# Forming the sixth input tile's products at a change of layer apart, as old input plus r times output, in an 18-sublayer transformer kernel

## What is computed

```
def rmsnorm(x, w):
    y = xf * rsqrt(mean(xf * xf, axis=-1) + NORM_EPS);  return y * w
def swiglu(x, w_in, w_out):
    g, u = split(x @ w_in, 2);  return (silu(g) * u) @ w_out
for i in range(DEPTH):
    h = h + 0.5 * rmsnorm(swiglu(rmsnorm(h, gn[0]), ffn1_w_in[i], ffn1_w_out[i]), gn[1])
    h = h + rmsnorm(mixer(rmsnorm(h, gn[2])), gn[3])
    h = h + 0.5 * rmsnorm(swiglu(rmsnorm(h, gn[4]), ffn2_w_in[i], ffn2_w_out[i]), gn[5])
```

## Time and profile before

| | us |
|---|---|
| median of 3 runs (lowest to highest) | 3103.48 (3103.17 to 3106.68) |
| the profiled execution's own time | 3105.66 |
| its span | 3103.9 |
| PE busy in the span | 3056.2 (98%) |
| DVE busy | 2252.3 (73%) |
| ACT busy | 1731.4 (56%) |

### The profile page before, as it was taken

One profiled execution on the slowest core, in us unless ns is written; L12 is line 12 of the kernel. 1 busy time (PEld: TensorE's weight loads), 2 busy tenths in 40 slices (PEclk: granted clock), 3 DMA queues, 4 the chain that ended last, 5 costly groups with the idle time before them and its releaser, 6 DMA issues.

```text
span 3103.9 us, 46097 instructions
## 1 busy us (share of the span) xinstructions
PE 3056.2 (98%) x18744; PEld 2702.2 (87%) x18744; DVE 2252.3 (73%) x2670; ACT 1731.4 (56%) x2092; POOL 4.1 (0%) x22
## 2 busy tenths in 40 slices
PE   9999999999999999899999999999999999999998
PEld 7888888888888888788888888888988888888887
DVE  7769775867786775685876977586777775867874
ACT  6556754645664654454655675464634654646653
POOL 0000000000000000000000000000000000000000
PEclk9999999999999999999999999999999999999999
DMA  6543455454355454355454345545433454554453
GB/s 229 188 172 140 157 188 182 179 189 164 135 187 188 173 188 171 143 188 189 176 190 176 136 152 188 189 177 190 175 138 107 177 188 168 192 190 161 163 190 122
DMA packets 75362, 534.87 MB, mean 172 GB/s; under 512 B 8480, under 2 KB 8608, under 8 KB 10784
## 3 DMA queue, kind: packets, MB, share of 16 engines
q1 hardware_dynamic: 75168, 532.07, 47.6%
HBM read 530.99 MB, written 1.05 MB: 171 GB/s over the span
## 4 chain that ended last, share of the span: by engine, by line
PE 93%; DVE 3%; ACT 2%; DMA 1%; issue 0%; DVEq 0%; SPq 0%; ACTq 0%
PE pp L2157 18%; PE pp L2156 18%; PE pp L2158 9%; PE pp L2155 9%; PE pp L2182 4%; PE pm L2157 4%; PE pm L2156 4%; PE pp L2148 3%; PE pp L2150 3%; PE pp L2149 3%; PE pp L2222 2%; PE pp L2184 2%; PE pm L2158 2%; PE pm L2155 2%; PE pp L2330 1%; PE pp L2212 1%
## 5 line engine op out<-in xcount | busy, mean ns | idle before, releaser
L1889 DVE TENSOR_TENSOR wlo<-raw,whi 128x2048 fp32r<-128x2048 f32 x487 | 1113.5, 2289 | 355.9 <-ACT whi L1682 355.2
L1682 ACT ACTIVATE whi<-raw 128x2048 fp32r<-128x2048 f32 x487 | 928.8, 1911 | 275.9 <-DMA raw<-weights 274.9
L2157 PE MATMUL pp<-xs,whi 128*128 128x512 f32 x2176 | 867.1, 398 | 1.9 <-DVE tsum L1969 1.7
L2156 PE MATMUL pp<-xs,whi 128*128 128x512 f32 x2176 | 860.8, 396 | 0.0
L2155 PE MATMUL pp<-xs,wlo 128*128 128x256 f32 x2176 | 605.8, 278 | 0.0
L2158 PE MATMUL pp<-xs,wlo 128*128 128x256 f32 x2176 | 603.6, 277 | 0.0
L1772 ACT ACTIVATE corr<-pp 128x512 f32<-128x512 f32 x320 | 191.0, 597 | 583.2 <-PE pp L2156 558.4
L2155 PEld LDWEIGHTS pp<-xs,wlo 128*128 128x128 f32 x2176 | 408.5, 188 | 99.4
L2158 PEld LDWEIGHTS pp<-xs,wlo 128*128 128x128 f32 x2176 | 409.2, 188 | 92.0
L2157 PEld LDWEIGHTS pp<-xs,whi 128*128 128x128 f32 x2176 | 413.1, 190 | 10.2 <-DVE tsum L1969 8.9
L2156 PEld LDWEIGHTS pp<-xs,whi 128*128 128x128 f32 x2176 | 407.8, 187 | 0.0
(11 more groups left out here) (387 smaller groups left out, 4762.8 us busy)
## 6 DMA issues: line engine op xcount, KB each, us to landing
raw<-weights SPq DMA_DIRECT2D x503, 1024.0 KB, 4.8
raw<-weights SPq DMA_DIRECT2D x8, 256.0 KB, 7.5
h<-x_by_feature SPq DMA_DIRECT2D x4, 256.0 KB, 6.6
out<-h SPq DMA_DIRECT2D x4, 256.0 KB, 2.5
vec<-vectors SPq DMA_DIRECT2D x1, 264.0 KB, 2.8
lamrow<-diff_lambda SPq DMA_DIRECT2D x1, 128.0 KB, 10.6
skiprow<-ssm_d SPq DMA_DIRECT2D x1, 8.0 KB, 12.0
```

Of the source, the lines that this page charges most:

```text
L1682: nc.scalar.activation(whi[:, slot, :], raw[:, slot, :], ACT.Copy).then_inc(sem("weights_hi"), 1)
L1889: v.tensor_tensor(wlo[:, slot, :], raw[:, slot, :], whi[:, slot, :].bitcast(F32), ALU.subtract).then_inc(sem("weights_lo"), 1)
L2156: return mm(bank, whi[:, slot, c:c + P], x_k, start=False, stop=stop)
L2157: mm(bank, whi[:, slot, c:c + P], x_k, start=start, stop=False)
```

## The change

- `fold`, a buffer in the place of `tsum`, takes the sixth tile (`APART` = 5) of the next sublayer's input in two pieces, each as high and low part: the gain times the old `h`, and the gain times the scaled output `upd`, before r is known. DVE makes the first in the old sublayer's read-out (`old_input`), the second after the last squares (`close_sublayer`).
- Behind the last column sum PE forms the old input's product straight into the in-banks of panels 0 and 1 (4 wide, 4 narrow) and the output's product into `pm` banks 0 and 1 (12 narrow). `keep_clock(5)` goes away except before the first sublayer. `first_pair` then adds tiles 0, 1, 2, 3, 4, 6, 7 to the banks; tile 5 is updated and split last.
- DVE adds r times the product from `pm` to the corrected panels 0 and 1 (`add_apart`), in two instructions for each panel.
- In every FFN's opening DVE's steps stand in another order: the split of panel 4 ahead of the first gate, the correction of panel 2 behind it, and the split of panel 6 behind the second hidden tile; on ACT the copy of panel 2 stands ahead of the first hidden tile.
- Pooling: the first group's product goes behind panel 3, the last group's behind the rows (2, 3). HGRN: the splits of the output panels 1 and 2 each one place ahead. The squares of tiles 6 and 7 are added before those of 4 and 5.

```diff
+        fold_offset = nc.sbuf_base
         tsum = sb("tsum", [P, 2, 2 * T])
+        fold = nc.alloc_sbuf_tensor_at("fold", [P, 2, 2 * T], F32R, offset=fold_offset)
+        APART = 5
+        TILES = (0, 1, 2, 3, 4, 6, 7, APART)
...
+            group(0)
             begin(s, 0)
             begin(s, 1)
             rows(s, (y,), (6, 7), ((0, 0), (0, 1), (1, 0), (1, 1)), order, scaled)
             group(1)
             group(2)
             rows(s, (y,), (4, 5), ((0, 0), (0, 1), (1, 0), (1, 1)), order, scaled)
+            rows(s, (y,), (2, 3), ((0, 0), (0, 1), (1, 0), (1, 1)), order, scaled)
             group(3)
-            rows(s, (y,), (2, 3), ((0, 0), (0, 1), (1, 0), (1, 1)), order, scaled)
...
             def hook(p):
                 steps_of(p)
+                if p == 13:
+                    split(s["segs"][1].g0 + 1)
                 if p == 14:
                     nc.scalar.preload_act_table_set("silu_and_others")
                     silu_of(range(3))
-                    split(s["segs"][1].g0 + 1)
+                    split(s["segs"][1].g0 + 2)
...
                 silu_of(0)
-                hidden_of(0)
                 for j in range(1, FF // PC):
                     g = seg.g0 + 2 * j
                     act.wait_ge(sem("panel_done"), g + 1)
                     copy_corr(in_banks[0], 0)
                     if j == 1:
+                        hidden_of(0)
                         split(g + AHEAD - 1)
...
+            def split_apart(s, part, src, ready):
+
+                src, gain = src[:, APART, :], vec[:, APART, s["gain"]:s["gain"] + 1]
+                v.tensor_scalar(fold[:, part, 0:T], src, gain, None, ALU.mult)
+                dve.drain()
+                v.scalar_tensor_tensor(fold[:, part, T:2 * T], src, gain, fold[:, part, 0:T].bitcast(F32),
+                                       ALU.mult, ALU.subtract).then_inc(sem(ready), 1)
...
                 output_squares(s, 1)
+                if nxt is not None:
+                    dve.wait_ge(sem("output_scaled"), 4 * n + APART // 2 + 1)
+                    split_apart(nxt, 1, upd, "output_split")
                 dve.wait_ge(sem("rstd_ready"), 2 * n + 2)
...
                 open_input(seg, s)
                 gate_of(0)
+                add_corr(t2[0], in_banks[0], 0, seg.c0 + 2)
+                if s["n"]:
+                    add_apart(1)
                 hidden_of(0)
-                split(seg.g0 + AHEAD)
                 hidden_lo(0)
                 for j in range(1, FF // PC):
                     g, c = seg.g0 + 2 * j, seg.c0 + 2 * j
-                    add_corr(t2[0], in_banks[0], 0, c)
+                    if j > 1:
+                        add_corr(t2[0], in_banks[0], 0, c)
                     dve.drain()
                     gate_of(j)
+                    split(g + AHEAD - (j == 1))
+                    add_corr(t2[1], in_banks[1], 1, c + 1)
+                    dve.drain()
+                    hidden_of(j)
                     if j == 1:
-                        split(g + AHEAD - 1)
-                    split(g + AHEAD)
-                    add_corr(t2[1], in_banks[1], 1, c + 1)
-                    dve.drain()
-                    hidden_of(j)
+                        split(g + AHEAD)
                     split(g + 1 + AHEAD)
                     hidden_lo(j)
+
+            def add_apart(p):
+
+                scale = rpost[:, :].rearrange("p (a t) -> p a t", a=1).to_broadcast([P, 2, T])
+                v.tensor_tensor(upd[:, 2 * p:2 * p + 2, :], two(pm[:, p, :]), scale, ALU.mult)
+                dve.drain()
+                v.tensor_tensor(t2[p], t2[p], upd[:, 2 * p:2 * p + 2, :], ALU.add)
+                dve.drain()
...
+                dve.drain()
+                if s["kind"] == FFN:
+                    split(seg.g0 + AHEAD)
+                if s["n"]:
+                    add_apart(0)
+                    if s["kind"] != FFN:
+                        add_apart(1)
...
+            def old_input(s):
+
+                if s["n"] + 1 < len(subs):
+                    split_apart(subs[s["n"] + 1], 0, h, "old_input_split")
...
+                tiles = TILES[:KD - 1] if fill else range(KD)
...
+                if fill:
+                    pe.wait_ge(sem("x_lo"), KD * fill + KD)
...
             def first_of(s):
 
-                keep_clock(5 if s["n"] else 7)
+                if s["n"] == 0:
+                    keep_clock(7)
                 first_pair(s["segs"][0], s["fill"])
...
+                seg = nxt["segs"][0]
+                pe.wait_ge(sem("weights_lo"), splits_before[seg.g0] + 2)
+                pe.wait_ge(sem("panel_out"), seg.r0)
+                pe.wait_ge(sem("output_scaled"), 4 * n + 3)
+                pe.wait_ge(sem("old_input_split"), n + 1)
+                old_input_product(nxt, 0)
+                pe.wait_ge(sem("output_scaled"), 4 * n + 4)
+                old_input_product(nxt, 1)
+                pe.wait_ge(sem("output_split"), n + 1)
+                output_product(nxt, 0)
+                output_product(nxt, 1)
```

More of the change, by code:

```diff
@@ L513, in pe_pool @@
             begin, rows, rest = out_products
+            products(s["segs"][0], xs, first=lambda: first_of(s), sums=lambda: column_sums(s), hook=lambda p: None)
             slot = seg.g0 % SLOTS
+            pe.wait_ge(sem(f"raw_landed_{slot}"), landings(seg.g0))
             def group(n):
@@ L527, in scaled @@
                 pe.wait_ge(sem("pool_scaled"), 4 - k // 2)
-            def first_group(p):
-                if p == 2:
-                    pe.wait_ge(sem(f"raw_landed_{slot}"), landings(seg.g0))
-                    group(0)
-            products(s["segs"][0], xs, first=lambda: first_of(s), sums=lambda: column_sums(s), hook=first_group)
+            group(0)
             begin(s, 0)
@@ L934, in act_hgrn @@
             hi_of(3)
-            split(s["segs"][1].g0 + 2)
             split(s["segs"][1].g0 + 3)
@@ L1721, in open_first @@
                         nc.scalar.activation(whi[:, g, quarter(c)], raw[:, g, quarter(c)], ACT.Copy).then_inc(sem("first_hi"), 1)
-                for q in (slice(0, 4), slice(4, 6), slice(6, 8)):
-                    if q.start == 6:
+                for q in (slice(0, 4), slice(6, 8), slice(4, 6)):
+                    if q.start == 4:
                         split(2)
@@ L1727, in open_sublayer @@
             def open_sublayer(s):
-                for k in range(1, KD):
-                    act.wait_ge(sem("h_ready"), KD * (s["n"] - 1) + k + 1)
+                for n, k in list(enumerate(TILES))[1:]:
+                    act.wait_ge(sem("h_ready"), KD * (s["n"] - 1) + n + 1)
                     nc.scalar.activation(xs[:, k, 0:T], h[:, k, :], ACT.Copy, scale=vec[:, k, s["gain"]:s["gain"] + 1]
@@ L1957, in close_sublayer @@
                 hi_of_tile_0(nxt)
-                lo_of_tile(nxt, 0)
+                lo_of_tile(nxt, 0, 0)
                 update(1)
-                for k in range(1, KD):
-                    if k < KD - 1:
-                        update(k + 1)
-                    lo_of_tile(nxt, k)
+                for place in range(1, KD):
+                    if place < KD - 1:
+                        update(TILES[place + 1])
+                    lo_of_tile(nxt, TILES[place], place)
                 dve.drain()
@@ L2040, in read_out @@
                     half, pair = (p + seg.first_half) % 2, p - seg.wide
+                    if closing and pair == 2:
+                        old_input(s)
                     if own_order and p in seg.tokens:
@@ L2181, in rows @@
                             if part == "whi":
-                                e = mm(bank, whi[:, slot, c:c + P], xs[:, k, :], start=(k == 0), stop=(k == KD - 1))
+                                e = mm(bank, whi[:, slot, c:c + P], xs[:, k, :], start=(k == 0 and not fill), stop=(k == KD - 1))
                             else:
@@ L2185, in rows @@
                     return e
-                for k in range(KD - 2):
+                for k in tiles[:-2]:
                     if fill == 0 and k % 2 == 0:
```

38 lines of the change are left out of this document (26 added, 12 removed).

## The result

The changed kernel takes **3143.16 us** (median of 4 runs, 3143.02 to 3145.0), the kernel before 3103.53 beside it: a ratio of 1.0127, 95% interval 1.0113 to 1.0140. It is slower, by 39.6 us. In its profiled execution it took 3143.03 us with a span of 3141.3, where the kernel before had 3105.66 and 3103.9: 37.4 us more in both.

The account below looks back on a forecast made before the run. PE bounds the kernel (93% of the chain); new PE waits for DVE are lost in full. FFNs 32.8, HGRN -1.5, pooling -3.4, REC +1.3, attention and HYB +0.2: +29.4 on 3103.48 gives 3132.9 us, range 3113 to 3147 (83%).

Parts of the forecast that it names:

- the opening FFN: First FFN: no pairs to add, loses only the split's place, which its slack takes; 0.
- The first tiles: At each sublayer change: added PE products replace constants at no cost; panel 2 comes 0.47 us sooner, the rest waits for DVE.
- The constants' rival: At sublayer changes: added products don't fit before 539.36 as a semaphore comes late; 0.5 us each, 17 times, 3141; 3%.
- The FFN's chain: FFN opening: DVE's pairs (1.54 us each) and moved split delay corrections 3 and 4; PE waits 1.88 and 1.57 us.
- Panel 6 starts at 576.94 and not at 573.96: In each FFN but the opening one: panel 6 starts 2.98 us later; times 11 is +32.8 us.
- Mixers: All get both pairs (3.08 us) before read-out: HGRN -1.5, pooling -3.4, REC +1.3, attention and HYB together +0.2.
- pooling: First group behind panel 3 waits 1.7 for 3.96 us, runs at full clock; smaller waits follow; -3.4 us.
- REC: Pairs add 3.08 us before a correction PE already waits for, less some 1.7 of DVE idle; +1.3 us.
- HGRN: PE up to 0.9 us late from the pairs; moved splits end a 1.68 us wait; -0.8 each, two: -1.5.
- The rival of the clock: PE's clock falls after the FFN's new 1.88 us wait, costing 1.26 us 11 times: 3147; 8%.
- the forecast's own signs of being wrong: Correction waits totalling under 20 us (38 forecast), granted clock falling inside an FFN, or pairs outside 1.4 to 1.6 us.
- The skill's shorter pair: DVE's pairs: by the skill page's fixed cycles, a pair 0.13 us shorter, the sum some 3 us lower; not adopted.

Follow-up runs that it names:

- without pairs: The changed kernel without the two pairs of DVE instructions (scale the output's product, add it) in the 11 FFNs, mixers keeping theirs: 3109.04 us (1.0017).
- the order alone: The kernel before with only the changed order of DVE and ACT in the FFN's opening, nothing computed apart: 3114.52 us (1.0035).
- the run without their pairs: The changed kernel without the two pairs of DVE instructions in the 6 mixers, the FFNs keeping theirs: 3131.16 us (1.0092).
- the moves alone: The kernel before with only pooling's first and last groups and HGRN's splits moved as in the change: 3094.52 us (0.9970).

## Why the prediction was right

The forecast was 3132.9 in a range of 3113 to 3147 with slower at 86%; it came to 3143.2. The direction and the mechanism were right, the size 10 us short. Of these, 3.9 are in the FFNs and 4.6 in the mixers, against 0.5 won at the start and in the opening FFN; the remaining 2.2 are no work: the forecast took the profiled execution as 2.2 above the median, and the changed kernel's is not.

- **The first tiles: right.** Added products fit before the low part; PE's wait there fell to 0.27, the wait at panel 2 is 0.9, as said. The constants' rival fell. By medians the parts add up so: FFN pairs 34.1, mixer pairs 12.0, order 10.7, moves -9.9; the measured 39.6 leaves -7.3 for the first tiles, 0.43 at each of 17 changes (0.47 in the forecast). This is what is left over, no run has it by itself, and the even share is in part luck: in the FFNs panel 6 comes 0.56 sooner without pairs than with the order alone (34.59 and 35.15 below), and in the mixers the run without their pairs against that of the moves alone gives 0.3 on average, with nothing to speak of in attention and REC.
- **The FFN's chain: right, nearly to the step.** Counted from the first matmul, the correction of panel 0 comes at 10.37 (10.39 foretold), of panel 3 at 29.67 (29.69), of panel 4 at 36.84 (36.84). The wait at panel 5 is 1.8 (1.88). A pair takes 1.60 and 1.52 us with its drains (559.56 to 561.16, 563.64 to 565.16), and 1.5 in the runs without it (1.54).
- **"Panel 6 starts at 576.94 and not at 573.96": two small slips, +2.98 against +3.34.** PE's timeline of the kernel before, at panel 6, and of the changed one at panel 6 of the FFN that opens at 2035.55, where the clock stayed up:

```profile
573.79 0.39 PE L2157 MATMUL pp<-xs,whi 128*128 128x512 f32 x1
574.03 0.28 PE L2158 MATMUL pp<-xs,wlo 128*128 128x256 f32 x1
...
2073.08 0.50 PE L2197 MATMUL pp<-xs,whi 128*128 128x512 f32 x1 [1.32 <-DVE tsum L1982]
2073.42 0.28 PE L2198 MATMUL pp<-xs,wlo 128*128 128x256 f32 x1
```

 I had taken panel 6's start from ACT's copy of panel 5 (573.96). PE itself begins it at 573.79, before that copy, since it has no need to wait for its own last matmul to end: 34.43 us after the FFN's first matmul. In the changed kernel it is 37.53, so +3.10. And the first matmul behind a wait starts its follower 0.34 us later, where 0.23 is the rule: +0.11. Together 3.21, and 3.15 to 3.26 is what the undisturbed FFNs show. The same two explain the runs: the order alone has panel 6 at 35.15, +0.72 + 0.11 = 0.83 (0.8 measured), without pairs 34.59, +0.27 (0.26). A wait that the profile calls 0.56 costs 0.83. Over 11 FFNs this is 2.5 us. Five FFNs take another 0.1 to 0.4 us, 1.5 us together: in three of them DVE's corrections of panels 3 and 4 come 0.36 later, in a fourth that of panel 5, and each of the four has one idle time of 0.43 to 0.46 on DVE that the profile calls issue (before 1053.49, 1345.02, 1857.73 and 2965.66). The fifth has none in its opening, and its 0.1 stays open. The forecast had seen that some FFNs differ by 0.4; it cost nothing while DVE had slack, and I had let it go.
- **Mixers: the sum failed.** -3.4 was forecast, +1.2 came, 4.6 us. These are pooling, and REC's DVE, then PE:

```profile
1264.89 1.96 PE L528 MATMUL pm<-mix,raw 128*128 128x256 f32 x8 [1.54 <-DVE mix L498]
1268.08 3.69 PE L2402 MATMUL pp<-y,raw 128*128 128x256 f32 x16 [1.23 <-DVE tsum L1982]
...
2867.54 1.48 DVE L2112 TENSOR_TENSOR mix<-tsum,rpre 128x512 f32<-128x512 f32 x2 [0.18 <-issue]
...
2874.16 0.69 DVE L1982 TENSOR_TENSOR tsum<-pp,corr 128x512 f32<-128x512 f32 x1 [1.01 <-ACT corr L1774]
...
2874.99 3.28 PE L410 MATMUL pp<-y,raw 128*128 128x256 f32 x7 [2.68 <-DVE tsum L1982]
```

 Pooling was near (-4.4 for -3.4; waits of 1.54 and 1.23 for 1.7 and 1.1), though the waits and the clock that the forecast lists give only -2.7, or -3.2 with the gain of the first tiles. REC: I took 1.7 us of idle as slack for the pairs. Only the idle before the factor was (0.69 before, 0.18 now). The 1.02 of the earlier trace rows stands there as before, 1.01: it ends with an ACT copy that itself comes after DVE's steps, so it moves with them. That is +2.3 on the correction, 2.68 of wait, and +2.0 for the sublayer, 0.7 above the forecast; the other 1.3 of its +3.3 are the half clock behind that wait. HGRN: with the gains of the moved splits taken out (0.95 and 1.33 in the run of the moves alone, where I had 1.68) the stalls are 1.2 and 2.6 us, for 0.9. The second has 0.81 us of its own on DVE that the first hasn't, right before the correction:

```profile
1716.37 0.73 DVE L990 TENSOR_SCALAR mix<-mix,lbw 128x256 f32<-128x256 f32 x2
```

 PE also waits 0.67 us in the second, 52.5 us after its first matmul (L1073, for DVE), where the first has no wait. I had laid out the first HGRN and doubled it.
- **The rival of the clock: its event came, its price only in REC.** The wait of 1.88 was "just beyond what is seen safe", and the clock fell in 7 of 11 FFNs. That was one of the forecast's own signs of being wrong; the others did not come (the waits for the corrections total 26.4 us, over 20, and a pair takes 1.5 to 1.6). They are 26.4 and not 38 mostly because the seven FFNs have no wait at panel 6: the half rate uses it up, and so the 1.26 us each did not appear there. Where no second wait followed, in REC, 1.3 us did. That the FFNs were spared was not foreseen, and the forecast owes its range to it: by an estimate, seven times 1.26 us more would have been 3152. The page "TensorE: Matmul & The Clock Gate" of the Trainium skill (section "Why this matters for your kernels") has idle gaps bring the half rate; the runs agree, and show it after waits of 1.8 to 2.2 us in seven of 11 cases, and after 3.4 us and more in ten of 11.
- **The skill's shorter pair: no.** By the page "VectorE: DVE Perf Modes" of the Trainium skill (section on the TRN2 errata) the read from PSUM would be the dearer one, and by an estimate from its figures the pair 0.13 us shorter. The trace does not agree: L2031 from PSUM takes 0.68, L2033 from SBUF 0.69.
- The time came out within 4 us of the clock's and the constants' rivals, 3147 and 3141, but for other reasons.

## What to carry to other kernels

Before work is taken from a waiting engine and given to another, lay out the second one's chain up to the next buffer that it frees: 1.5 us of pairs cost 1.5 us each, though DVE was busy for 74% of the span only. An idle gap is slack only if what ends it doesn't itself wait for the engine that idles, and work taken out of a chain can come back as idle time, as the order alone shows. A fall of the clock is paid only where no later wait takes it up. Of a change with several parts, time the parts that need no other: here two reorderings alone give 0.3%, and the rest loses 1.6% against them.
